# Recurrent gates in three split passes with their unit dealt anew, and four leading feed-forward pieces split ahead around the second norm

## The chip, the cores and the metric

The kernel runs on one core of one Trainium2 chip. The metric is the device time of that core in microseconds (us), the median of three runs. Engines are named as in the profile: PE is TensorE (matmul), PEld its weight loads, DVE VectorE, ACT ScalarE, POOL GpSimd and SP SyncE, which only starts DMAs here.

## The reference, cut to what matters

One layer over 256 tokens of width 2048, everything in fp32. A modulated RMSNorm feeds one input projection whose columns feed four token mixers. One of them is the recurrent unit (RG-LRU), computed for the tokens and for 256 context tokens, in both directions. The mixers are merged through sigmoid gates and one output projection. A second modulated RMSNorm follows, and then the feed-forward part.

```python
# recurrent unit: z is (tokens, 4 groups x 128), w_r and w_i are 4 blocks of 128x128 for each direction
r = sigmoid(block_diag_linear(z, w_r, b_r))
i = sigmoid(block_diag_linear(z, w_i, b_i))
log_a = -8.0 * r * softplus(-lam)
a = exp(log_a)
b = sqrt(-expm1(2.0 * log_a)) * (i * z)
h[t] = a[t] * h[t-1] + b[t]          # once forward, once backward

x_mixed = x + gt1 * (merged @ w_out)                          # out-projection, 2048 x 2048
h2 = (rms_norm(x_mixed) * g_ffn) * (1 + sc2) + sh2            # second norm
x = x_mixed + gt2 * ((silu(h2 @ w_ffn_gate) * (h2 @ w_ffn_up)) @ w_ffn_down)
```

## The kernel before, in words

**Split products.** PE multiplies fp32r operands. To keep fp32 accuracy every large operand is dealt into a high part (an ACT copy to fp32r) and a low part (a DVE subtraction, raw minus high), and each product is three passes: high by high, high by low, low by high (`rows3`, lines 1411 to 1413, and `piece_rows`, lines 1439 to 1441). Only small products, the recurrent gates among them, are plain fp32 matmuls (lines 1628 and 1629).

**Pieces.** All weights arrive in pieces of 256 x 512 (128 x 1024 on chip, 512 KB), numbered through the program. SP starts their DMAs into `RAW`, ACT writes `HI` (line 451, helper `high`), DVE writes `LO` (line 803, helper `low`). Each of the three buffers is a ring of four. `high(p)` waits for the landing and for PE to have finished piece p-4 (semaphore `used`), `low(p)` for `high(p)`, PE's piece p for `low(p)` (`ready`), and the DMA of piece p for `low(p-4)`. Small work is written into these streams by hand: `straight(w)` on ACT, DVE and PE is what comes behind piece w of the first 104. ACT and DVE work up to four pieces ahead of PE. An engine runs its stream in program order, so a wait holds back all that stands behind it.

**The recurrent unit.** For each of four groups g there is a unit placed at `LRU_AT[g]` (66, 73, 80, 87). DVE makes the convolution `Z` (a scale and three taps, 128x512 each) behind piece LRU_AT-3. PE runs four fp32 matmuls of 512 columns behind piece LRU_AT, two for each direction. ACT makes the sigmoids at +5 and +6, tanh and exp at +6 and +7, the square roots at +8 and +9. DVE makes i times z and two multiplications by (exp + 1) at +7 and +8 (lines 1058, 1060, 1061), the scans at +9 and +11, and the output is dealt by ACT at +12 and by DVE at +13.

**Around the second norm.** The out-projection is 32 pieces, eight (j = 0 to 7) for each of four column blocks n. In the last block, pieces j = 0 to 5 run for both token halves and pieces 6 and 7 first for half 0, then for half 1 (`row_pass`). `out_half` tells DVE that half 0 is complete. Then comes the chain of the norm for that half: DVE scales and adds the residual (`last_scaled`, `last_added`, lines 1216 and 1221), ACT squares the last 512 columns (line 706), DVE sums (1225), ACT takes the root (710), DVE takes the reciprocal and makes a diagonal (1229, 1230), and PE multiplies the residual stream by it, which turns and scales it at once (`h2_turn`, line 1803). The result is modulated and dealt in twelve units u: ACT's even column tile (718), DVE's odd one (1236, `h2_odd`), ACT's high part (721, `h2_high`), DVE's low part (903, `h2_low`). Units 0 to 3 are for token half 0 and units 4 to 7 for half 1 of the first eight column tiles; units 8 to 11 hold both halves of the other eight.

**The first feed-forward pieces.** I call pieces FFN0 to FFN0+15 f0 to f15; f0 to f7 are the gate weights of the first chunk. PE runs f0 to f3 by token halves, with `h2_turn` in between, and then f4 to f15 for both halves. Piece f4 waits for `h2_low` of unit 8, f5 for unit 9, f6 for unit 10 and f7 for unit 11 (PE waits for `h2_lo` at least w+5). In the streams of ACT and DVE, piece and unit are interlaced. For w = 4 to 9, DVE runs the odd part of unit w+2, the low part of piece fw and the low part of unit w+2; ACT runs `high(fw)` and then `h2_high(w+2)`. So the units stand two ahead of the pieces.

**What runs beside it.** POOL streams the modulation matrix, and DVE multiplies and adds its rows (line 915).

Of the kernel before, what the change touches and what calls it, by code (L numbers as in the profile page):

```python
# [104 lines left out]
LRU_AT = (66, 73, 80, 87)  # L105

# [27 lines left out]
def build(nc, x, c, ctx, c_ctx, w_mod, b_mod, g_mix, g_ffn, g_final, w_in, w_pool, pool_scale,  # L134
# [3 lines left out]
    with ctxs:  # L138
# [12 lines left out]
        Y = H[:, 0, :, :, :]  # L151
        HID = H[:, 0, 0:G4, :, :]
        HIDL = H[:, 0, G4:2 * G4, :, :]
        SUMS_HI = [[H[:, 0, 8 * g + n, :, :].rearrange("p l t -> p (l t)") for n in range(4)] for g in range(2)]
        SUMS_LO = [[H[:, 0, 8 * g + 4 + n, :, :].rearrange("p l t -> p (l t)") for n in range(4)] for g in range(2)]
# [58 lines left out]
        HS = BR[:, 11360:11616]  # L214
# [65 lines left out]
        def _(sp):  # L280
# [76 lines left out]
            for t in range(2):  # L357
                for n in (1, 0, 2, 3):
                    if n:
                        sp.wait_ge(s("rows_dve"), 3 * t + n)  # L360
                    else:
                        sp.wait_ge(s("rows_act"), t + 1)
                    sp.dma_start(out[0, t * P:(t + 1) * P, n * BW:(n + 1) * BW], OTOK[:, n, t, :]).then_inc(s(f"stored{t}"), 16)
            for t in range(2):
                sp.wait_ge(s(f"stored{t}"), 64)
# [77 lines left out]
        def _(act):  # L443
# [9 lines left out]
            act.dma_start(CST[:, :], cst).then_inc(s("cst_in"), 16)  # L453
            act.dma_start(CROW[0:KT, :], c[0].rearrange("(a n) -> a n", n=P)).then_inc(s("crow_in"), 16)
            act.dma_start(CROW[KT:2 * KT, :], c_ctx.rearrange("(a n) -> a n", n=P)).then_inc(s("crow_in"), 16)
# [106 lines left out]
            def straight(w):  # L562
# [43 lines left out]
                if w == SMALL_MM + 5:  # L606
                    act.wait_ge(s("sgu_float"), 1)
                    act.activation(Y[:, 4:8, 0, :], YF, ACT.Copy).then_inc(s("sgu_hi"), 1)
                if w == 70:
# [3 lines left out]
                for g in range(G4):  # L613
                    if w in (LRU_AT[g] + 5, LRU_AT[g] + 6):
                        for d in (w - LRU_AT[g] - 5,):
# [7 lines left out]
                            act.activation(LT[:, d, 0, :], ps[:, 4 + 2 * d, :], ACT.Sigmoid, bias=PB[:, PB_BR + col:PB_BR + col + 1]).then_inc(s("lru_r"), 1)  # L623
                            act.activation(LT[:, d, 1, :], ps[:, 5 + 2 * d, :], ACT.Sigmoid, bias=PB[:, PB_BI + col:PB_BI + col + 1]).then_inc(s("lru_i"), 1)
                    if w in (LRU_AT[g] + 6, LRU_AT[g] + 7):
                        for d in (w - LRU_AT[g] - 6,):
# [3 lines left out]
                            act.activation(LT[:, d, 2, :], LT[:, d, 0, :], ACT.Tanh, scale=LRC[:, 6, col:col + 1]).then_inc(s("lru_t"), 1)  # L630
                            act.activation(LT[:, d, 3, :], LT[:, d, 0, :], ACT.Exp, scale=LRC[:, 7, col:col + 1]).then_inc(s("lru_e"), 1)
# [4 lines left out]
                    if w == LRU_AT[g] + 12:  # L636
# [48 lines left out]
            def sums_high(g, n, src, groups):  # L685

                act.wait_ge(s("mod_used"), groups * KT + 2)
                act.activation(SUMS_HI[g][n], src, ACT.Copy).then_inc(s("sums_hi"), 1)

# [33 lines left out]
            high(FFN0 // 4, 0)  # L723
            high(FFN0 // 4, 1)
# [3 lines left out]
            high(FFN0 // 4, 2)  # L728
# [24 lines left out]
            for w in range(10, 16):  # L753
                high(FFN0 // 4, w)
                if w == 11:
                    ffn_gate(0, FFN0 + 7)
# [40 lines left out]
        def _(dve):  # L797
# [20 lines left out]
            dve.wait_ge(s("cst_in"), 16)  # L818
# [109 lines left out]
            def straight(w):  # L928
# [122 lines left out]
                for g in range(G4):  # L1051
                    if w in (LRU_AT[g] + 7, LRU_AT[g] + 8):
                        z = Z[:, g % 2, :]
                        for d in (w - LRU_AT[g] - 7,):
# [3 lines left out]
                            own.did(tt(I, I, z, ALU.mult))  # L1058
                            dve.wait_ge(s("lru_e"), n + 1)
                            own.did(stt(TH, EA, 1.0, TH, ALU.add, ALU.mult)); own.wait()  # L1060
                            stt(TH, EA, 1.0, TH, ALU.add, ALU.mult).then_inc(s("lru_w"), 1)
                    if w in (LRU_AT[g] + 9, LRU_AT[g] + 11):
                        for d in ((w - LRU_AT[g] - 9) // 2,):
                            n = 2 * g + d
                            R, I, TH, EA = (LT[:, d, k, :] for k in range(4))
                            dve.wait_ge(s("lru_s"), n + 1)
# [896 lines left out]
```

## Time and profile before

| | us |
|---|---|
| runs: median of 3 (lowest, highest) | 1635.61 (1634.35, 1636.22) |
| the profiled execution, its own time | 1635.51 |
| its span, first to last instruction | 1633.8 |
| PE busy in the span | 1603.9 |
| DVE busy | 1103.1 |
| ACT busy | 730.8 |

The 1.7 us between the execution's own time and its span lie around the span. A matmul is pipelined: a row gives its start and its whole latency, and the distance between the starts of neighbours is what it costs in a full stream.

### The profile page before, as it was taken

Reading aid. Unit: us, or ns where it says so; the run is one execution under the profiler, and the core shown is the slowest. Engines: PE = TensorE matmul, PEld = TensorE weight load, DVE = VectorE, ACT = ScalarE, POOL = GpSimd, SP = SyncE. Lnnn points to the kernel's source line nnn. Section 1 sums busy time; section 2 is a strip of 40 time slices with the busy share of each in tenths; the row PEclk is TensorE's granted clock in tenths of the full one; section 3 lists DMA queues with packets and bytes.
Section 4 is the critical chain, followed back from the end, with each engine's and each line's share of the span. In section 5 each row is a group of like instructions: output and inputs, shape, how many; then the busy total and the mean of one; then the engine's idle time right before and its main releaser. Section 6 shows DMA issues by size and latency. Waiting matters only on the chain.

```text
span 1633.8 us, 22715 instructions
## 1 busy us (share of the span) xinstructions
PE 1603.9 (98%) x7899; PEld 1322.8 (81%) x7899; DVE 1103.1 (68%) x1271; ACT 730.8 (45%) x820; POOL 159.6 (10%) x296
## 2 busy tenths in 40 slices
PE   6999999999999999999999999999999999999998
PEld 4678798987788888888887888888888888888886
DVE  4333556878888888877896576867755556456577
ACT  5333234468744444444445544443444444434444
POOL 1002111000022122123020010101100000000000
PEclk9999999999999999999999999999999999999999
DMA  9998746645589889899685677878776666666654
GB/s 346 356 357 245 243 144 203 222 147 156 187 298 326 282 297 337 278 340 341 220 287 164 179 235 244 280 233 268 248 254 193 191 193 187 188 191 191 190 174 139
DMA packets 200545, 390.28 MB, mean 239 GB/s; under 512 B 14400, under 2 KB 47408, under 8 KB 199584
## 3 DMA queue, kind: packets, MB, share of 16 engines
q1 hardware_dynamic: 176960, 312.51, 59.7%
q0 software_dynamic: 23312, 76.79, 14.1%
q8 instruction: 40, 0.66, 0.2%
q14 instruction: 25, 0.20, 0.0%
q10 hardware_dynamic: 208, 0.11, 0.0%
HBM read 386.35 MB, written 3.01 MB: 238 GB/s over the span
## 4 chain that ended last, share of the span: by engine, by line
PE 90%; DMA 5%; DVE 2%; issue 1%; ACT 1%; SPq 0%; POOL 0%; POOLq 0%; DVEq 0%; ACTq 0%
PE ps L1439 24%; PE ps L1441 24%; PE ps L1440 24%; PE ps L1411 5%; PE ps L1412 4%; PE ps L1413 4%; DMA BR<-in_w_mod 4%; PE ps L1407 2%; PE ps L1492 1%; DVE BR L915 1%; DMA MR<-in_w_mod 1%; DVE LO L803 1%; PE ps L1603 0%; PE ps L1590 0%; PE ps L1629 0%
## 5 line engine op out<-in xcount | busy, mean ns | idle before, releaser
L803 DVE TENSOR_TENSOR LO<-RAW,HI 128x1024 fp32r<-128x1024 f32 x519 | 633.0, 1223 | 399.5 <-ACT HI L451 398.3
L451 ACT ACTIVATE HI<-RAW 128x1024 fp32r<-128x1024 f32 x519 | 548.4, 1060 | 751.9 <-PE ps L1441 626.2
L1439 PE MATMUL ps<-HI,H 128*128 128x512 f32 x1840 | 720.6, 392 | 1.4 <-DVE ATT L1110 1.0
L1441 PE MATMUL ps<-HI,H 128*128 128x512 f32 x1840 | 716.4, 389 | 0.0
L1440 PE MATMUL ps<-LO,H 128*128 128x512 f32 x1840 | 716.0, 389 | 0.0
L1439 PEld LDWEIGHTS ps<-HI,H 128*128 128x128 f32 x1840 | 345.5, 188 | 74.5 <-DVE ATT L1110 1.4
L1441 PEld LDWEIGHTS ps<-HI,H 128*128 128x128 f32 x1840 | 345.4, 188 | 72.2
L1440 PEld LDWEIGHTS ps<-LO,H 128*128 128x128 f32 x1840 | 345.6, 188 | 72.0 <-issue 1.2
L413 POOL DMA_DIRECT2D BR<-in_w_mod x224 | 120.4, 538 | 765.2 <-DVE BR L915 306.4
L915 DVE SCALAR_TENSOR_TENSOR BR<-BR,SCF 128x512 f32<-128x512 f32 (+1 forms) x210 | 156.7, 746 | 12.7 <-DMA BR<-in_w_mod 10.8
L1411 PE MATMUL ps<-H,HI 128*128 128x256 f32 (+1 forms) x384 | 125.7, 327 | 0.1
L1412 PE MATMUL ps<-H,HI 128*128 128x256 f32 (+1 forms) x384 | 122.9, 320 | 0.0
L1413 PE MATMUL ps<-H,LO 128*128 128x256 f32 (+1 forms) x384 | 122.7, 320 | 0.0
L1411 PEld LDWEIGHTS ps<-H,HI 128*128 128x128 f32 x384 | 73.4, 191 | 11.0 <-issue 5.4
L1412 PEld LDWEIGHTS ps<-H,HI 128*128 128x128 f32 x384 | 73.5, 191 | 5.3 <-issue 0.2
L1413 PEld LDWEIGHTS ps<-H,LO 128*128 128x128 f32 x384 | 73.4, 191 | 5.3
L1289 DVE TENSOR_TENSOR ATT<-ps,ATT 128x1024 f32<-128x1024 f32 x36 | 43.8, 1216 | 0.0
L1411 PE MATMUL ps<-HI,H 128*128 128x512 f32 x80 | 32.3, 404 | 2.0 <-DVE H L903 2.0
L1492 PE MATMUL ps<-BR 128*32 128x256 f32 x400 | 26.7, 384 | 5.4 <-DMA BR<-in_w_mod 5.4
L1412 PE MATMUL ps<-LO,H 128*128 128x512 f32 x80 | 31.3, 391 | 0.0
L1413 PE MATMUL ps<-HI,H 128*128 128x512 f32 x80 | 31.2, 390 | 0.0
L1407 PE MATMUL ps<-CST,BR 128*128 128x128 f32 (+1 forms) x129 | 19.4, 303 | 11.7 <-DMA BR<-in_c_ctx 8.5
(258 smaller groups left out, 759.2 us busy)
## 6 DMA issues: line engine op xcount, KB each, us to landing
RAW<-in_w_gate SPq DMA_DIRECT2D x128, 512.0 KB, 4.7
BR<-in_w_mod POOLq DMA_DIRECT2D x224, 256.0 KB, 4.6
RAW<-in_w_ffn_gate SPq DMA_DIRECT2D x88, 512.0 KB, 3.8
RAW<-in_w_ffn_up SPq DMA_DIRECT2D x88, 512.0 KB, 3.7
RAW<-in_w_ffn_down SPq DMA_DIRECT2D x88, 512.0 KB, 3.7
RAW<-in_w_in SPq DMA_DIRECT2D x64, 512.0 KB, 5.7
BR<-in_w_mod SPq DMA_DIRECT2D x50, 512.0 KB, 9.4
RAW<-in_w_branch SPq DMA_DIRECT2D x32, 512.0 KB, 5.2
```

Source lines behind the costliest of these rows:

```text
L413: pool.dma_start(slots[:, k % ring, :], w_mod[0, k * P:(k + 1) * P, bass.ds(g * BW + first, BW)])\
L451: act.activation(HI[:, j % RING, :], RAW[:, j % RING, :], ACT.Copy).then_inc(hi_done, 1)
L803: tt(LO[:, j % RING, :], RAW[:, j % RING, :], HI[:, j % RING, :], ALU.subtract).then_inc(lo_done, 1)
L915: i = stt(acc, src, SCF[:, 0, k:k + 1], acc, ALU.mult, ALU.add)
L1289: tt(flat(ACC[:, n, :]), pair(4 + 2 * (n % 2)), flat(ACC[:, n, :]), ALU.add).then_inc(s("down_read"), 1)
L1407: return mm(o, src, IDENT[0:n, 0:n], start=start, stop=True, is_transpose=True, skip_group_check=True)
L1411: mm(o, wh, xh, start=first, stop=False, skip_group_check=True)
L1412: mm(o, wh, xl, start=False, stop=False, skip_group_check=True)
L1413: return mm(o, wl, xh, start=False, stop=last, skip_group_check=True)
L1439: mm(o, xh, wh, start=first and t == 0, stop=False, skip_group_check=True)
L1440: mm(o, xh, wl, start=False, stop=False, skip_group_check=True)
L1441: i = mm(o, xl, wh, start=False, stop=last and t == 1, skip_group_check=True)
```

## The change: what it does

1. **Gates in three passes.** The weights of the gates are dealt into high (ACT, behind pieces 53, 55, 56 and 59, one group of 128x512 each) and low (DVE, four pieces later). `Z` of each unit is dealt too: high by ACT at LRU_AT-2, low by DVE at LRU_AT-1. PE runs `rows3` in place of each fp32 matmul, and waits for both low parts.
2. **The unit dealt anew.** The convolution moves to LRU_AT-6 (scale, first tap) and LRU_AT-4 (two taps). ACT takes the root right behind the tanh, without waiting for DVE. DVE then multiplies by (exp + 1) once, at +9 and +10, in place of twice. The output is dealt one piece later (+13, +14).
3. **Pieces f0 to f3 ahead.** They are dealt out of `RAW` into eight free rows of `H` (`AHEAD_HI`, `AHEAD_LO`) and not into the ring, so that they no longer wait for ring slots. Then f4 to f7 take the ring slots as the pieces of the out-projection leave them (`high_behind`).
4. **Token halves.** The last four pieces of the out-projection (j = 4 to 7) run by token halves, not the last two, and the first `h2_turn` stands behind piece 6 of the second half.
5. **Order of ACT and DVE behind that.** Written anew, see the diff: for u = 8 to 11, unit u and then piece fu.
6. Some semaphores are merged: DVE's first reduction waits for three constants' DMAs and not for one, and SP's last waits are one.

```diff
+LRU_SPLIT_AT = (53, 55, 56, 59)
...
+        GATES_HI = Y[:, 8:12, :, :].rearrange("p g l (h n) -> p g l h n", h=2)
+        ROWS = [H[:, 0, k, :, :].rearrange("p l t -> p (l t)") for k in range(KT)]
+        AHEAD = [H[:, 0, k:k + 2, :, :].rearrange("p k l t -> p (k l t)") for k in (8, 10, 12, 14, 2, 4, 6, 0)]
+        AHEAD_HI, AHEAD_LO = AHEAD[0::2], AHEAD[1::2]
...
# ACT, straight(w)
+                if w in LRU_SPLIT_AT:
+                    g = LRU_SPLIT_AT.index(w)
+                    act.wait_ge(s("small_in"), 16 * 7)
+                    act.wait_ge(used, 8 * 3 + 8 + 4)
+                    act.activation(GATES_HI[:, g], GATES[:, g], ACT.Copy).then_inc(s("gates_hi"), 1)
+                if w + 2 in LRU_AT:
+                    g = LRU_AT.index(w + 2)
+                    act.wait_ge(s("conv"), g + 1)
...
+                    act.activation(ZH, Z[:, g % 2, :], ACT.Copy).then_inc(s("conv_hi"), 1)
...
-                            act.wait_ge(s("lru_w"), 2 * g + d + 1)
+                            act.wait_ge(s("lru_t"), 2 * g + d + 1)
                             act.activation(LT[:, d, 2, :], LT[:, d, 2, :], ACT.Sqrt).then_inc(s("lru_s"), 1)
...
# ACT, second norm
-            high(FFN0 // 4, 0)
-            high(FFN0 // 4, 1)
+            def high_ahead(w):
+                act.wait_ge(landed[w], FFN0 // 4 * 16 + 16)
+                if w == 2:
+                    act.wait_ge(s("gate1_spread"), 1)
+                act.activation(AHEAD_HI[w], RAW[:, w, :], ACT.Copy).then_inc(hi_done, 1)
+            def high_behind(w):
+                act.wait_ge(landed[w % RING], FFN0 // 4 * 16 + 32)
+                act.wait_ge(used, FFN0 + w - 3)
+                act.activation(HI[:, w % RING, :], RAW[:, w % RING, :], ACT.Copy).then_inc(hi_done, 1)
+            for w in range(4):
+                high_ahead(w)
             act.activation(ST[:, 62:63], EPSC[:, 0:1], ACT.Sqrt)
             square_last(0)
             root(0)
-            high(FFN0 // 4, 2)
+            high_behind(4)
             act.wait_ge(s("a2"), 1)
             h2_high(0)
             h2_high(1)
-            high(FFN0 // 4, 3)
+            square_last(1)
             h2_high(2)
-            square_last(1)
+            root(1)
             h2_high(3)
-            root(1)
+            high_behind(5)
             h2_high(4)
             h2_high(5)
-            for w in range(4, 10):
-                high(FFN0 // 4, w)
-                h2_high(w + 2)
+            high_behind(6)
+            h2_high(6)
+            high_behind(7)
+            h2_high(7)
+            for u in range(8, 12):
+                h2_high(u)
+                high(FFN0 // 4, u)
...
# DVE, straight(w)
-                            own.did(tt(I, I, z, ALU.mult))
+                            tt(I, I, z, ALU.mult).then_inc(s("lru_w"), 1)
+                    if w in (LRU_AT[g] + 9, LRU_AT[g] + 10):
...
                             own.did(stt(TH, EA, 1.0, TH, ALU.add, ALU.mult)); own.wait()
-                            stt(TH, EA, 1.0, TH, ALU.add, ALU.mult).then_inc(s("lru_w"), 1)
...
+                if w - 4 in LRU_SPLIT_AT:
+                    g = LRU_SPLIT_AT.index(w - 4)
+                    split_low("gates_hi", g + 1, GATES_LO[:, g], GATES[:, g], GATES_HI[:, g], "gates_lo")
+                if w + 1 in LRU_AT:
...
+                    split_low("conv_hi", g + 1, ZL, Z[:, g % 2, :], ZH, "conv_lo")
...
# DVE, second norm
+            def low_ahead(w):
+                dve.wait_ge(hi_done, FFN0 + w + 1)
+                if w >= 2:
+                    dve.wait_ge(s("gate1_spread"), w - 1)
+                tt(AHEAD_LO[w], RAW[:, w, :], AHEAD_HI[w], ALU.subtract).then_inc(lo_done, 1)
-            low(FFN0, 0)
-            low(FFN0 + 1, 1)
+            low_ahead(0)
+            low_ahead(1)
             last_scaled(0)
             last_added(0)
+            low_ahead(2)
             squares_summed(0)
             rstd_diagonal(0)
+            low_ahead(3)
             h2_odd(0)
             h2_odd(1)
             h2_low(0)
-            h2_odd(2)
             h2_low(1)
-            low(FFN0 + 2, 2)
             last_scaled(1)
             last_added(1)
+            h2_odd(2)
+            h2_odd(3)
             h2_low(2)
-            h2_odd(3)
-            low(FFN0 + 3, 3)
             squares_summed(1)
             h2_low(3)
             rstd_diagonal(1)
-            for u in (4, 5):
+            low(FFN0 + 4, 4)
+            low(FFN0 + 5, 5)
+            for u in (4, 5, 6, 7):
                 h2_odd(u)
                 h2_low(u)
-            for w in range(4, 10):
-                h2_odd(w + 2)
-                low(FFN0 + w, w)
-                h2_low(w + 2)
+                if u >= 6:
+                    low(FFN0 + u, u)
+            for u in range(8, 12):
+                h2_odd(u)
+                h2_low(u)
+                low(FFN0 + u, u)
...
# PE
-                            mm(ps[:, 4 + 2 * d, :], SW[:, 8 + 4 * d + g, :], Z[:, g % 2, :], start=True, stop=True)
-                            mm(ps[:, 5 + 2 * d, :], SW[:, 16 + 4 * d + g, :], Z[:, g % 2, :], start=True, stop=True)\
+                            rows3(ps[:, 4 + 2 * d, :], GATES_HI[:, g, 0, d, :], GATES_LO[:, g, 0, d, :], ZH, ZL, True, True)
+                            rows3(ps[:, 5 + 2 * d, :], GATES_HI[:, g, 1, d, :], GATES_LO[:, g, 1, d, :], ZH, ZL, True, True)\
                                 .then_inc(s("lru_mm"), 1)
...
-                for j in range(8 if n < 3 else 6):
+                for j in range(8 if n < 3 else 4):
...
             for q in range(2):
-                for j in (6, 7):
-                    i = row_pass(OUT0 + 24 + j, j, tokens_of(HX), q, ps[:, 2 + q, :], 2 * j, False, j == 7)
+                for j in range(4, 8):
+                    i = row_pass(OUT0 + 24 + j, HI[:, j % RING, :], LO[:, j % RING, :], tokens_of(HX), q, ps[:, 2 + q, :],
+                                 2 * j, False, j == 7)
+                    if q and j == 6:
+                        h2_turn(0)
                 if q == 0:
-                    i.then_inc(s("out_half"), 1)
-
-            h2_turn(0)
+                    i.then_inc(s("half_done"), 1)
+
             h2_turn(1)
```

## Rows read from the trace of the kernel before

**Rows 1.** The page, part 1: busy time, share of the span, instructions.

```profile
PE 1603.9 (98%) x7899; PEld 1322.8 (81%) x7899; DVE 1103.1 (68%) x1271; ACT 730.8 (45%) x820; POOL 159.6 (10%) x296
```

**Rows 2.** Waits of PE over the span: us in total, times, longest.

```profile
PE ps L1407 <- DMA BR<-in_c_ctx: 8.5, 1, 8.5
PE ps L1411 <- DVE H L903: 2.0, 4, 0.6
PE ps L1439 <- DVE ATT L1110: 1.0, 1, 1.0
```

**Rows 3.** Chain of waits around the first recurrent unit: start, us, what.

```profile
344.98 0.86 PE ps L1628 x2
348.41 0.23 PE ps L1439
```

**Rows 4.** Timeline of ACT, DVE and PE behind piece f4.

```profile
908.71 0.39 PE L1439 MATMUL ps<-HI,H 128*128 128x512 f32 x1
908.97 1.06 ACT L451 ACTIVATE HI<-RAW 128x1024 fp32r<-128x1024 f32 x1 [2.02 <-PE ps L1441]
910.06 1.23 DVE L803 TENSOR_TENSOR LO<-RAW,HI 128x1024 fp32r<-128x1024 f32 x1 [1.78 <-ACT HI L451]
911.20 0.68 DVE L903 TENSOR_TENSOR H<-BR,H 128x512 fp32r<-128x512 f32 x1
911.80 0.54 DVE L1236 TENSOR_SCALAR BR<-ps,A,MC 128x256 f32<-128x256 f32 x1
911.94 0.50 PE L1439 MATMUL ps<-HI,H 128*128 128x512 f32 x1 [0.35 <-DVE H L903]
913.23 0.63 ACT L721 ACTIVATE H<-BR 128x512 fp32r<-128x512 f32 x1
914.82 0.39 PE L1439 MATMUL ps<-HI,H 128*128 128x512 f32 x1
917.54 0.39 PE L1439 MATMUL ps<-HI,H 128*128 128x512 f32 x1
```

**Rows 5.** Groups by line, DVE, 340 to 440 us: busy, mean ns, idle.

```profile
L1061 DVE SCALAR_TENSOR_TENSOR ATT<-ATT 128x512 f32<-128x512 f32 x8 | 5.5, 692 | 0.3
```

**Rows 6.** Timeline before the units: start, us, line, [idle and who ended it].

```profile
315.39 2.35 DVE L803 TENSOR_TENSOR LO<-RAW,HI 128x1024 fp32r<-128x1024 f32 x2
318.98 1.06 ACT L451 ACTIVATE HI<-RAW 128x1024 fp32r<-128x1024 f32 x1 [1.82 <-PE ps L1413]
```

**Rows 7.** Timeline of DVE, ACT and PE from the end of the out-projection to piece f4.

```profile
873.99 1.23 DVE L803 TENSOR_TENSOR LO<-RAW,HI 128x1024 fp32r<-128x1024 f32 x1 [1.96 <-ACT HI L451]
879.41 1.28 ACT L725 ACT_TABLE_LOAD   x1
881.00 0.69 DVE L1216 TENSOR_TENSOR ATT<-ps,ACCM 128x512 f32<-128x512 f32 x1 [0.34 <-PE ps L1413]
882.44 0.63 ACT L706 ACTIVATE ATT<-BR 128x512 f32<-128x512 f32 x1 [1.53 <-DVE BR L1221]
884.26 2.05 PE L1803 MATMUL ps<-ATT,BR 128*128 128x128 f32 x16 [0.58 <-DVE ATT L1230]
905.86 0.47 PE L1439 MATMUL ps<-HI,H 128*128 128x512 f32 x1
```

**Rows 8.** The page, part 6: DMA issues, size, us from issue to landing.

```profile
RAW<-in_w_ffn_gate SPq DMA_DIRECT2D x88, 512.0 KB, 3.8
```

**Rows 9.** Windows: PE, PEld, DVE, ACT, POOL busy (count), PE clock, DMA, GB/s.

```profile
883.52:905.86 22.34, 19.75 (x113) 16.10 (x113) 15.18 (x31) 14.54 (x29) 0.00 (x0) 1.00 0.34 97
28.00:32.00 4.00, 1.25 (x12) 0.71 (x12) 2.42 (x7) 2.77 (x6) 0.00 (x0) 1.00 1.07 360
32.00:36.00 4.00, 3.65 (x15) 2.61 (x16) 2.51 (x3) 1.78 (x3) 0.00 (x0) 0.60 1.10 351
```

**Rows 10.** Chain of waits where the clock was low: start, us, what.

```profile
34.20 0.43 PE ps L1413
```

**Rows 11.** Timeline of DVE at the start.

```profile
8.86 0.16 DVE L874 RECIPROCAL ST<-ST 128x1 f32<-128x1 f32 x1 [1.99 <-ACT ST L493]
```

More of the change, by code:

```diff
@@ L362, in _ @@
                         sp.wait_ge(s("rows_act"), t + 1)
-                    sp.dma_start(out[0, t * P:(t + 1) * P, n * BW:(n + 1) * BW], OTOK[:, n, t, :]).then_inc(s(f"stored{t}"), 16)
-            for t in range(2):
-                sp.wait_ge(s(f"stored{t}"), 64)
+                    sp.dma_start(out[0, t * P:(t + 1) * P, n * BW:(n + 1) * BW], OTOK[:, n, t, :]).then_inc(s("stored"), 16)
+            sp.wait_ge(s("stored"), 128)
         @block.gpsimd
@@ L1081, in straight @@
                         tt(HS, HS, LG[:, g * T:g * T + T], ALU.mult).then_inc(s("lru_float"), 1)
-                    if w == LRU_AT[g] + 13:
+                    if w == LRU_AT[g] + 14:
                         split_low("lru_hi", g + 1, Y[:, 8 + g, 1, :], HS, Y[:, 8 + g, 0, :], "lru_lo")
-                if w + 3 in LRU_AT:
-                    g = LRU_AT.index(w + 3)
-                    z = Z[:, g % 2, :].rearrange("p (s t) -> p s t", s=2)
-                    dve.wait_ge(s("win_read"), 2)
-                    if g == 0:
-                        dve.wait_ge(s("pooled"), 1)
-                    if g >= 2:
-                        dve.wait_ge(s("lru_w"), 2 * (g - 1))
-                    own.did(ts(z, LP[:, g, :, 0:T], PB[:, PB_CW + g:PB_CW + g + 1], PB[:, PB_CB + g:PB_CB + g + 1], ALU.mult, ALU.add))
-                    for k in range(1, CONV):
+                if w - 4 in LRU_SPLIT_AT:
+                    g = LRU_SPLIT_AT.index(w - 4)
+                    split_low("gates_hi", g + 1, GATES_LO[:, g], GATES[:, g], GATES_HI[:, g], "gates_lo")
+                if w + 1 in LRU_AT:
+                    g = LRU_AT.index(w + 1)
+                    if g:
+                        dve.wait_ge(s("lru_mm"), 2 * g)
+                    else:
+                        dve.wait_ge(s("sgu_mm"), 1)
+                    split_low("conv_hi", g + 1, ZL, Z[:, g % 2, :], ZH, "conv_lo")
+                for g in range(G4):
+                    if w not in (LRU_AT[g] - 6, LRU_AT[g] - 4):
+                        continue
+                    z = Z[:, g % 2, :].rearrange("p (s t) -> p s t", s=2)
+                    if w == LRU_AT[g] - 6:
+                        dve.wait_ge(s("win_read"), 2)
+                        if g == 0:
+                            dve.wait_ge(s("pooled"), 1)
+                        if g >= 2:
+                            dve.wait_ge(s("lru_w"), 2 * (g - 1))
+                        own.did(ts(z, LP[:, g, :, 0:T], PB[:, PB_CW + g:PB_CW + g + 1], PB[:, PB_CB + g:PB_CB + g + 1], ALU.mult, ALU.add))
+                        taps = (1,)
+                    else:
+                        taps = (2, 3)
+                    for k in taps:
                         own.wait()
@@ L1164, in sums_low @@
             def sums_low(g, n, src):
+                if g == 0 and n == 3:
+                    dve.wait_ge(s("gate1_spread"), 1)
                 split_low("sums_hi", 4 * g + n + 1, SUMS_LO[g][n], src, SUMS_HI[g][n], "sums_lo")
@@ L1363, in _ @@
                 if w == 21:
-                    dve.memset(ST[:, 3:4], EPS).then_inc(s("eps_set"), 1)
-                    dve.memset(ST[:, 7:8], EPS).then_inc(s("eps_set"), 1)
+                    own.did(dve.memset(ST[:, 3:4], EPS))
+                    own.did(dve.memset(ST[:, 7:8], EPS))
                 if w == 25:
@@ L1386, in last_rows @@
                     dve.wait_ge(s("sqf"), 6)
-                    dve.wait_ge(s("eps_set"), 2)
+                    own.wait()
                     for u in range(2):
@@ L1776, in gate1_spread, with row_pass @@
                 i.then_inc(s("gate1_spread"), 1)
-            def row_pass(p, j, lhs, q, o, k0, first, last):
+            def row_pass(p, hi, lo, lhs, q, o, k0, first, last):
                 ready(p)
                 for t in range(2):
-                    wh, wl = HI[:, j % RING, t * BW:(t + 1) * BW], LO[:, j % RING, t * BW:(t + 1) * BW]
+                    wh, wl = hi[:, t * BW:(t + 1) * BW], lo[:, t * BW:(t + 1) * BW]
                     xh, xl = lhs(k0 + t, q)
```

63 lines of the change are left out of this document (38 added, 25 removed).

## The prediction

> **What bounds the kernel now.** I read the page first. PE is busy 98% of the span, DVE 68%, ACT 45% [rows 1], and the chain of waits is 90% PE. So whatever PE is spared, and whatever wait is put in front of it, shows in the time nearly one to one; work of ACT and DVE counts only where PE waits for it. Next the list of PE's waits: behind the first 60 us there is hardly one, except around the second norm, where PE waits for DVE's line 903 (low parts of units), four times, 2.0 us in all [rows 2]. That is the place the change rewrites. Last I read the timelines of ACT, DVE and PE side by side there, since both streams are written by hand and run in order: what a stream waits for matters as much as how long its work takes.
>
> **Gates in three passes.** A unit of four fp32 matmuls takes 348.41 - 344.98 = 3.43 us, 0.86 each [rows 3]. An fp32r pass of 512 columns in a full stream costs 2.72 us / 12 = 0.227 us (914.82 to 917.54 is one piece of 12 matmuls) [rows 4]. A unit becomes 12 passes: 2.72 us, 0.71 less. Four units: -2.8 us. All of it is on PE's path. Both ends: the twelve passes may cost 0.23 to 0.24 each where weights change every pass, so -2.2 to -2.9.
>
> **What the dealing costs.** DVE gets eight subtractions of 128x512 (gates and Z) and loses eight multiplications of the same size at 0.69 us [rows 5]: even. ACT gets eight copies, each like its square of 128x512, 0.63 us [rows 7], where it idles 1 to 2 us behind each piece. The tight place is before the units, where pooling and normalization keep DVE late: the low parts of pieces 59 and 60 end at 317.7 (315.39 + 2.35), the first of them at 316.5, and PE takes piece 59 up at 318.9, when piece 58 is done [rows 6]. In front of piece 59 the change puts one subtraction (0.6 us): the lead falls from 2.4 to 1.7 us and holds. Two more and the first half of the convolution (some 1.3 us) come in front of piece 61, where PE arrives two pieces later. I take 0; if the cover fails, some tenths, up to 1 us. Inside the units the root no longer waits for DVE and the low part of Z is written several pieces ahead: 0. The output is dealt one piece later, with several pieces to spare before the fourth branch group.
>
> **The end of the out-projection.** Half 0 is complete two half passes earlier, 2 x 1.36 = 2.7 us, so DVE's residual can start at 878.3 in place of 881.0 [rows 7]. The chain of the norm then waits for something else: ACT's stream. Four early high parts now stand in front of the table load. The fourth needs the DMA of f3, which starts when the low part of the last out-projection piece is written, 873.99 + 1.23 = 875.2 [rows 7], and lands 3.8 us later at 879.0 [rows 8]. Then 1.1 for the high part, 1.28 for the table load and 0.2 for its instruction: the square comes at 881.7, not 882.44, 0.75 earlier. From square to turn is 884.26 - 882.44 = 1.82 [rows 7], so `h2_turn` starts at 883.5. But PE stands before it at 882.2 (883.5 less the half pass that was moved behind it) and waits 1.3 us where it waited 0.7. That pass then covers the first units. I follow the streams down to f4 with a half pass at 1.36 (0.1 more behind a wait), a turn group of the norm at 0.85, and the durations of ACT and DVE in these rows: turn 883.5, half pass 884.4, turn 885.8, f0 886.6; f2 waits 0.9 for unit 2, which stands behind the residual and the square of half 1, until 890.4; f3 waits 0.2, until 892.1; the turns of half 1 from 893.6; f0 of half 1 waits 0.9 for unit 4 (two low parts of pieces stand before it in DVE's queue), until 896.2; a turn from 899.0, f2 900.7, the last turn 903.6, f4 905.3, where the trace has 905.86: -0.6. The stretch has 22.34 - 19.75 = 2.6 us in which PE is idle [rows 9]; that is the most the step can win. It can lose about 1. I take -0.6.
>
> **Pieces f4 to f7, the step that decides.** Ring slot 0 holds f4, so the high part of f8 can't be written before PE is done with f4. Before, DVE's order was odd part of unit w+2, low part of piece w, low part of unit w+2: when DVE stood waiting for f8, unit 9 was long dealt and unit 10 half done. So f5 found its unit ready, and f6 (unit 10) waited 0.5 us: 911.94 against 911.43 [rows 4]. Now the order is unit u, then piece fu. DVE writes unit 8 and then waits for f8, hence for the end of f4; unit 9 stands behind it in the queue. PE, done with f4, needs unit 9 for f5. ACT has the same order. The same repeats: unit 10 stands behind f9 (end of f5), unit 11 behind f10 (end of f6). So PE waits a full chain before f5, f6 and f7. The chain, from the instant when PE could start the next piece (908.71 in the trace) [rows 4]: 0.26 to the high part of f8 (908.97), 1.09 to its low part (910.06), 1.14 until DVE is free (911.20), the odd part of the unit 0.54, a handover of 0.1, ACT's high part 0.63, 0.03, DVE's low part 0.68, 0.06 to PE. Sum 4.53 us. Nothing hides any link, since each waits for the one before it and the first waits for PE itself.
>
> From f4 to f8 before: 917.54 - 905.86 = 11.7 us. After: 2.85 for f4, three times (4.53 + 2.88), the piece with its slower first pass: 25.1. The difference is +13.4 for this stretch. The 2.88 is f6 behind its wait, 914.82 - 911.94 [rows 4]. Both ends: each wait 4.2 to 4.8, so +12.4 to +14.2. Behind f8 the high and low parts of f8 to f10 exist already and the streams catch up within two pieces: 0.
>
> **PE's clock in these waits.** The trace has one loss of clock after the start. In the window 28 to 32 us PE is busy 1.25 us of 4, and in the next one the granted clock is 0.60 on average [rows 9], that is 1.2 GHz for some 3 us: seven matmuls start 0.43 us apart [rows 10], not 0.227, a loss of 7 x 0.2 = 1.4 us. The idle stretches of 0.6 to 1.8 us elsewhere cost no clock. The new waits, 4.3 us of idle, lie between, nearer to the one that did. Bounds: 0, or one such loss for each wait, 4.2, or, if the 2.8 us pieces between waits do not bring it back, 12 x 0.2 + 12 x 0.2 + 1.4 = 6.2. I take 1.8, a bit more than one loss. The Trainium skill, "TensorE: Matmul & The Clock Gate", section "HAM oscillation — how this bites in real kernels", describes this pattern: short bursts between waits of this length each start on the low clock, every time. By that rule the term is 4.2 or more and the time about 1650. No run here shows it for waits of 4.3 us.
>
> **Elsewhere.** PE's one other wait of the long middle, 1.0 us for line 1110 [rows 2], ends a stage in which DVE waits for the modulation stream; that chain starts from PE's own pieces, so it moves with them: 0, give or take 0.5.
>
> **Start and end.** DVE's first reduction now waits for the constants that PE waits for until 8.47 [rows 2]; it takes 0.2 us, and DVE's next instruction is at 8.86 anyway [rows 11]. I take 0, at most 0.2. SP's last wait: 0.
>
> **Sum.** Against the profiled execution (1635.5 us of its own, 1.7 of it around the span; the median of the runs is 1635.6, so no correction): -2.8 - 0.6 + 13.4 + 1.8 = +11.8. Time 1647.3.
>
> **Rivals.**
> The clock falls in every wait (the rule above, as a mechanism of this kernel: f5, f6 and f7 each begin at 1.2 GHz): -2.8 - 0.6 + 13.4 + 4.2 = +14.2, 1649.7; with no recovery inside a piece 1651.7. For it: 4.3 us of idle. Against: the one fall in the trace came after 5 us that were nearly empty.
> The waits before f5 to f7 don't exist (the other side, faster). Its place is DVE's queue at unit 9: it decides from the point where unit 9 to 11 are dealt before PE ends f4, which needs them ahead of the piece in program order. Then only the gains remain, and the 0.6 of f6 too: -2.8 - 0.6 - 0.6 = -4.0, 1631.5. For it: the ahead pieces do free ACT and DVE by about 3 us before f4. Against: the order in the code; time alone can't help, as the wait is for PE.
> The gate unit gives nothing: its passes wait for a low part, or the lead before piece 59 is lost. The gain of 2.8 goes, the waits stay: 1650.1. Against: leads of several pieces.
> The waits are partly hidden and the gains larger, which together end near no change (1635 to 1641). I see no cover for a wait that is for PE itself.
>
> **Chances.** Forecast (three chains, clock lost in part, 1645.5 to 1649) 0.62; clock lost in all 0.17; gates give nothing 0.10; faster 0.06; near no change 0.05, of which 0.03 is within 0.2%. 0.2% is 3.3 us, about what a measurement of this kernel can tell. Faster 0.06, same 0.03, slower 0.91. Range 1642 to 1652.
>
> **What the profile will show.** Right: three idle stretches of PE of about 4.2 us before f5, f6 and f7, ended by line 903 of DVE, each with ACT's high part starting 0.1 us after PE stopped; units of recurrent gates 2.7 us long; no wait of PE between 290 and 440 us; `h2_turn` at a wait of about 1.3. The granted clock between f5 and f8 says which clock case holds. Wrong: if f5 starts right behind f4, my reading of the order is wrong and the time is below 1633.

## The result, and the profile after

| | us, median of the runs | ratio to before, 95% interval |
|---|---|---|
| before | 1635.91 (1634.35 to 1637.9) | |
| after | 1651.39 (1650.78 to 1655.12) | 1.0099 (1.0087 to 1.0111) |

The ratios here and below are estimated from all the runs and need not be the quotients of the medians. By the medians the kernel became slower by 15.5 us. The forecast was 1647.3, with 1642 to 1652 as its range. The profiled execution after took 1651.08 us with a span of 1649.4, so the spans differ by 15.6 us and can be compared directly.

The page's first part, after (busy time, share of the span, instructions; answers to [rows 1]):

```profile
PE 1607.7 (97%) x7915; PEld 1329.3 (81%) x7915; DVE 1103.5 (67%) x1271; ACT 734.3 (45%) x828; POOL 159.6 (10%) x296
```

PE is still the bound, with one per cent of the span lost. The list of PE's waits, after (who waited for whom: us in total, times, longest; answers to [rows 2]). Lines have moved: line 944 was 903 (low part of a unit), 844 was 803 (low part of a piece), 1511 to 1513 are the three passes of a piece for both token halves, 1483 to 1485 the passes of `rows3`, 1875 is the norm's turn. Kernels of the experiments with added lines shift these numbers again by one to five (the first pass of a piece is line 1513 in e2 and 1516 in e1):

```profile
PE ps L1511 <- DVE H L944: 13.1, 3, 4.4
PE ps L1483 <- DVE H L944: 1.2, 2, 0.6
PE ps L1483 <- DVE LO L844: 0.9, 1, 0.9
PE ps L1875 <- DVE ATT L1292: 0.8, 1, 0.8
```

The first row is new: three waits of 4.4 us. The second is what is left of the four waits of 2.0 us in all. The third is new as well, and the 1.0 us for line 1110 is gone; of these two more is said below.

PE's timeline behind piece f4, after (start, us, line, operation, [idle and who ended it]; answers to [rows 4]):

```profile
901.78 0.48 PE L1511 MATMUL ps<-HI,H 128*128 128x512 f32 x1
...
904.37 0.39 PE L1513 MATMUL ps<-HI,H 128*128 128x512 f32 x1
909.12 0.80 PE L1511 MATMUL ps<-HI,H 128*128 128x512 f32 x1 [4.37 <-DVE H L944]
909.72 0.63 PE L1512 MATMUL ps<-LO,H 128*128 128x512 f32 x1
910.14 0.63 PE L1513 MATMUL ps<-HI,H 128*128 128x512 f32 x1
...
913.98 0.63 PE L1513 MATMUL ps<-HI,H 128*128 128x512 f32 x1
918.98 0.79 PE L1511 MATMUL ps<-HI,H 128*128 128x512 f32 x1 [4.37 <-DVE H L944]
...
928.84 0.80 PE L1511 MATMUL ps<-HI,H 128*128 128x512 f32 x1 [4.37 <-DVE H L944]
...
931.99 0.41 PE L1512 MATMUL ps<-LO,H 128*128 128x512 f32 x1
...
933.15 0.39 PE L1511 MATMUL ps<-HI,H 128*128 128x512 f32 x1
```

Read it in two passes. First the brackets: f5, f6 and f7 each begin behind 4.37 us of idle that DVE's low part of their unit ended. Then the starts: behind a wait the passes are 0.427 us apart (909.72, 910.14), not 0.227. In f5 and f6 it stays so to the end of the piece; in f7 it ends after three microseconds.

The chain of waits between f4 and f5, after (start, us, what):

```profile
904.53 0.24 PE ps L1513
...
904.85 1.06 ACT HI L459
905.94 1.23 DVE LO L844
907.17 0.47 DVE BR L1298
...
907.72 0.64 ACT H L746
908.38 0.70 DVE H L944
...
909.12 0.80 PE ps L1511
```

This is the sum of the prediction, link by link: PE's end frees the ring slot, ACT writes the high part of f8, DVE its low part, then DVE the odd part of unit 9, ACT its high part, DVE its low part. The same links follow f5 (from 914.71) and f6 (from 924.56).

Windows of the stretch, after (busy us and counts of PE, PEld, DVE, ACT, POOL; granted clock; DMA; GB/s):

```profile
909.00:914.00 5.00, 4.88 (x12) 3.81 (x12) 0.07 (x1) 0.00 (x0) 0.00 (x0) 0.50 0.22 82
...
919.00:924.00 5.00, 5.00 (x12) 3.77 (x12) 0.00 (x0) 0.00 (x0) 0.00 (x0) 0.50 0.24 89
...
929.00:934.00 5.00, 5.00 (x16) 4.01 (x17) 0.00 (x0) 0.59 (x1) 0.00 (x0) 0.70 0.19 73
```

The clock column is 0.50 while f5 and f6 run, that is 1.2 GHz, and PE is 98 to 100% "busy" in them. The same 12 matmuls take 5.3 us there and 2.9 us in [rows 4]; the busy column alone would not show it.

Two windows inside the idle stretch between f5 and f6, after (PE busy and count; clock; DMA; GB/s):

```profile
915.00:918.00 3.00, 0.00 (x0) 1.00 0.00 0
918.00:918.50 0.50, 0.00 (x0) 0.83 1.26 102
```

The last pass of f5 ended at 914.6 by the profile. The granted clock is full again from 915.0 on, with PE idle, and falls once more before f6 starts. So f6 is not slow because the low clock was carried over from f5: each wait loses the clock anew, and it came back too late to serve f5. It is the same between f6 and f7.

Where the 15.6 us came from, by the start of the same work on PE in both traces:

| stretch, by its end on PE | after minus before, us |
|---|---|
| four recurrent units, 0.65 each | -2.6 |
| before piece 55, a wait that was not there | +1.0 |
| the wait for line 1110, which is gone, and small change | -1.4 |
| end of the out-projection to f4 | -1.1 |
| f4 to f8: 31.37 (901.78 to 933.15) against 11.68 [rows 4, 7] | +19.7 |
| sum | +15.6 |

Of the 19.7 the waits are 13.4: a wait costs 4.52 us (the pass of 0.227 behind 904.37 would have been followed at 904.60, and f5 came at 909.12). The low clock is 6.3: f5 and f6 each 5.29 us (909.12 to 914.41, which is 913.98 and one step of 0.427) where 2.88 is the piece at full clock with its slower first pass, and f7 4.31 (928.84 to 933.15). 2.41 + 2.41 + 1.43 = 6.25.

### The profile page after: what moved, and what is told of

Same layout as the page of the kernel before. It is cut to its first block, busy times and chain, and to the rows that moved or that the text cites. A ratio compares the mean times of both kernels' runs of the same rounds, so it can differ in the third digit from the quotient of the medians.

```text
span 1649.4 us, 22782 instructions
## 1 busy us (share of the span) xinstructions
PE 1607.7 (97%) x7915; PEld 1329.3 (81%) x7915; DVE 1103.5 (67%) x1271; ACT 734.3 (45%) x828; POOL 159.6 (10%) x296
## 4 chain that ended last, share of the span: by engine, by line
PE 93%; DMA 3%; ACT 2%; DVE 1%; issue 0%; SPq 0%; DVEq 0%; POOLq 0%; ACTq 0%
PE ps L1511 25%; PE ps L1513 25%; PE ps L1512 25%; PE ps L1483 4%; PE ps L1485 4%; PE ps L1484 4%; PE ps L1479 1%; DMA MR<-in_w_mod 1%; PE ps L1563 1%; DMA BR<-in_w_mod 1%; PE ps L1674 0%; PE ps L1661 0%; DVE LO L844 0%; ACT ATT L498 0%; PE ps L1875 0%
## 5 line engine op out<-in xcount | busy, mean ns | idle before, releaser
L459 ACT ACTIVATE HI<-RAW 128x1024 fp32r<-128x1024 f32 x511 | 540.3, 1060 | 764.2 <-PE ps L1513 651.0
L1511 PE MATMUL ps<-HI,H 128*128 128x512 f32 x1832 | 718.6, 392 | 13.1 <-DVE H L944 13.1
L1513 PE MATMUL ps<-HI,H 128*128 128x512 f32 x1832 | 715.6, 391 | 0.0
L1512 PE MATMUL ps<-LO,H 128*128 128x512 f32 x1832 | 715.4, 390 | 0.0
L421 POOL DMA_DIRECT2D MR<-in_w_mod x32 | 17.5, 549 | 117.1 <-DVE ACCM L956 103.2
L956 DVE SCALAR_TENSOR_TENSOR ACCM<-MR,SCF,ACCM 128x512 f32<-128x512 f32 x30 | 22.4, 748 | 9.5 <-DMA MR<-in_w_mod 9.5
L1483 PE MATMUL ps<-HI,H 128*128 128x512 f32 x72 | 28.6, 398 | 0.0
```

The costliest lines, as they stand in the source:

```text
L421: pool.dma_start(slots[:, k % ring, :], w_mod[0, k * P:(k + 1) * P, bass.ds(g * BW + first, BW)])\
L459: act.activation(HI[:, j % RING, :], RAW[:, j % RING, :], ACT.Copy).then_inc(hi_done, 1)
L956: i = stt(acc, src, SCF[:, 0, k:k + 1], acc, ALU.mult, ALU.add)
L1483: mm(o, wh, xh, start=first, stop=False, skip_group_check=True)
L1511: mm(o, xh, wh, start=first and t == 0, stop=False, skip_group_check=True)
L1512: mm(o, xh, wl, start=False, stop=False, skip_group_check=True)
```

## The experiments

e1 to e4 compare with 27 runs of the kernel before, median 1635.82 us, e5 to e8 with 15 runs of it on another chip, 1635.53. They stand here in the order of their questions, behind the row of the kernel after from above.

| kernel | us, median | ratio, 95% interval | stretch of the second norm |
|---|---|---|---|
| after | 1651.39 | 1.0099 (1.0087 to 1.0111) | unit u, then piece fu |
| e1 | 1634.32 | 0.9992 (0.9983 to 1.0002) | units one ahead of the pieces |
| e2 | 1631.36 | 0.9975 (0.9966 to 0.9984) | units 8 to 11 ahead of f8 to f11 |
| e3 | 1646.05 | 1.0062 (1.0046 to 1.0077) | as after, waits filled, 18 matmuls each |
| e7 | 1645.34 | 1.0060 (1.0041 to 1.0078) | as after, 8 matmuls in each wait |
| e8 | 1651.48 | 1.0097 (1.0079 to 1.0116) | as after, 4 matmuls in each wait |
| e4 | 1633.19 | 0.9981 (0.9972 to 0.9990) | as before; the gates of the change |
| e6 | 1632.30 | 0.9980 (0.9971 to 0.9989) | e2, fewer token halves |
| e5 | 1629.41 | 0.9961 (0.9948 to 0.9975) | e2, the norm's chain first |

### Is it the order, and how far ahead must a unit be? (e1, e2)

The theory: f5 to f7 wait since their unit is queued behind a piece that waits for PE. The rival: DVE and ACT have too much to do in this stretch, and would be late in any order. e2 deals the four units first; nothing is added or removed. In ACT's stream, and alike in DVE's:

```diff
             for u in range(8, 12):
                 h2_high(u)
+            for u in range(8, 12):
                 high(FFN0 // 4, u)
```

> The changed kernel with units 8 to 11 all ahead of pieces f8 to f11 on ACT and DVE. My theory: no wait before f5, f6 and f7, the stretch f4 to f8 is 10.9 to 11.1 us, no fall of the clock, the high part of f8 is late by nothing that PE sees. Time 1651.4 - 20.3 = 1631.1, faster than the kernel before (1635.9) by 4.8. Rival (DVE's load decides): four units one behind the other take DVE and ACT over 5 us, f5 or f6 waits 1 to 3 us, time 1633 to 1635.

1631.36 us: 20.0 below the kernel after by moving loop bodies. PE's timeline of e2, first passes of f4, f5 and f6:

```profile
903.10 0.48 PE L1513 MATMUL ps<-HI,H 128*128 128x512 f32 x1
...
905.91 0.39 PE L1513 MATMUL ps<-HI,H 128*128 128x512 f32 x1
...
908.63 0.39 PE L1513 MATMUL ps<-HI,H 128*128 128x512 f32 x1
```

There is no bracket and each piece follows 2.72 us behind the last. The granted clock is 1.00 from 904 to 934 us. The rival is out: both engines have the time. e1 puts each unit one piece ahead only (unit 9, f8, unit 10, f9, unit 11, f10):

```diff
+            h2_high(8)
-            for u in range(8, 12):
+            for u in range(9, 12):
                 h2_high(u)
-                high(FFN0 // 4, u)
+                high(FFN0 // 4, u - 1)
+            high(FFN0 // 4, 11)
```

> The changed kernel with one edit: on ACT and DVE the units stand one ahead of the pieces (unit 8, unit 9, f8, unit 10, f9, unit 11, f10, f11). My theory (the three waits come from the order unit u, then piece fu, as f8 needs the end of f4, and the low clock comes from these waits): no wait before f5; before f6 one chain less the piece f5, 4.5 - 2.7 = 1.8 us; before f7 none. The stretch f4 to f8 is 10.9 + 1.8 + 0.1 = 12.8 us, not 31.4, and the clock stays at 2.4 GHz, since 1.8 us of idle cost no clock elsewhere. Time 1651.4 - 18.6 = 1632.8. Rival (the units are late because DVE has too much to do there, not because of the order): the waits go down by less than half and the time stays above 1642.

1634.32 us, 1.5 above what was expected, and too near the kernel before for its interval to tell them apart (0.9983 to 1.0002). PE's timeline of e1 has one wait that the theory gave (1.8 expected; 909.75 stands in place of 907.94, so 1.81) and one that it did not:

```profile
909.75 0.50 PE L1516 MATMUL ps<-HI,H 128*128 128x512 f32 x1 [1.66 <-DVE H L946]
...
913.14 0.50 PE L1516 MATMUL ps<-HI,H 128*128 128x512 f32 x1 [0.37 <-DVE H L946]
```

ACT's timeline of e1 tells why (the high part of f9):

```profile
908.88 1.04 ACT L459 ACTIVATE HI<-RAW 128x1024 fp32r<-128x1024 f32 x1
```

PE ended f5 at 907.94 (its last pass started at 907.71), but ACT stood in the high part of unit 10 and took up f9 at 908.88, 0.94 us later. The chain to unit 11 then took 4.26 us more and ended at 913.14, where PE would have been at 912.6. The expectation had started the second chain from PE's end alone; the first chain's delay is handed on. With its slower first passes the second wait accounts for 0.7 of the 1.5 us; the rest stays open (the spans of the profiled executions of e1 and e2 differ by 1.9 us, the medians by 3.0). A lead of one piece hides 2.7 us of a chain of 4.5, a lead of all four hides it.

### Is the rest of the loss the clock? (e3, e7, e8)

After, the three waits stand beside a loss of 6.3 us in slow pitch. The theory: that is the clock, lost by idleness, so work without use in the wait brings it back while the wait keeps its length. The rival: a pass behind such a wait is slow for another reason (weight loads, data that comes late), and filling changes nothing.

```diff
             for w in range(4, 16):
+                if w in (5, 6, 7):
+                    pe.wait_ge(s("xm_new"), 5)
+                    for _ in range(18):
+                        mm(ps[:, 2, :], HX[:, 0, 0, 0:P], AHEAD_HI[0][:, 0:BW], start=True, stop=True, skip_group_check=True)
```

> The changed kernel with 18 matmuls of 512 columns into an unused bank in front of each of PE's three waits (before f5, f6 and f7); their results aren't used. The waits stay as long as they were, but PE works in them. My theory (the clock falls because PE stands idle 4.4 us, and that costs 6.3 us): f5 to f7 run at 0.227 us a pass, the time falls by some 6 us to 1645.2, a sum of -2.6 (gates), -1.1, -1.4 and +13.6 (three waits) against the kernel before. Rival (the clock is a state of its own there, or the work of these pieces runs slow for another reason): no change, 1651.4, or slower by the added work.

1646.05 us, 5.3 below the kernel after. Its profiled execution was the longest of its four (1648.39), with 1.9 us of waiting in the modulation stage, so its rows are read and its span is not. PE's timeline of e3:

```profile
908.17 4.24 PE L1920 MATMUL ps<-H 128*128 128x512 f32 x18
912.71 0.50 PE L1511 MATMUL ps<-HI,H 128*128 128x512 f32 x1 [0.30 <-DVE H L944]
913.05 0.40 PE L1512 MATMUL ps<-LO,H 128*128 128x512 f32 x1
913.29 0.40 PE L1513 MATMUL ps<-HI,H 128*128 128x512 f32 x1
```

The wait is as long as before (4.5 us from the end of the piece) and the pitch behind it is 0.24, not 0.43. The rival is out. e7 and e8 have 8 and 4 matmuls in place of 18, to see how much idleness it takes.

> The changed kernel with 8 matmuls in front of each of PE's three waits (in e3 there were 18), so that PE stands idle about 2.6 us in each. Two readings of the clock: if an idle stretch of 2.6 us keeps it, as those of up to 1.8 us do in the kernel before, the time is that of e3, 1645.5 to 1646; if it falls, f5 to f7 start at 1.2 GHz and the time is up to 6 us longer, to 1651.4. I expect the first, 1646.

> The same with 4 matmuls: idle about 3.5 us in each wait. 1646 if the clock stays, 1651.4 if it falls in all three, between them if in some. I expect that it falls in some, 1648.5.

e7, PE's timeline at the first wait and the window behind it (PE's columns alone: busy, count, clock, DMA, GB/s):

```profile
905.03 1.98 PE L1920 MATMUL ps<-H 128*128 128x512 f32 x8
909.57 0.50 PE L1511 MATMUL ps<-HI,H 128*128 128x512 f32 x1 [2.56 <-DVE H L944]
909.90 0.39 PE L1512 MATMUL ps<-LO,H 128*128 128x512 f32 x1
```

```profile
909.00:914.00 5.00, 4.43 (x19) 1.00 0.31 102
```

e8, the same views, with the first passes behind the second and the third wait:

```profile
906.05 1.07 PE L1920 MATMUL ps<-H 128*128 128x512 f32 x4
910.58 0.79 PE L1511 MATMUL ps<-HI,H 128*128 128x512 f32 x1 [3.47 <-DVE H L944]
911.17 0.63 PE L1512 MATMUL ps<-LO,H 128*128 128x512 f32 x1
...
920.43 0.79 PE L1511 MATMUL ps<-HI,H 128*128 128x512 f32 x1 [3.27 <-DVE H L944]
...
930.29 0.79 PE L1511 MATMUL ps<-HI,H 128*128 128x512 f32 x1 [3.11 <-DVE H L944]
```

```profile
909.00:914.00 5.00, 3.42 (x8) 0.55 0.36 105
```

In the second and third wait of e8 the added matmuls began at the low clock and got it back before they ended, at about 916.3 and 926.5, and it fell again. e7 is at 1645.34, with all three waits at full clock; e8 at 1651.48, the time of the kernel after, with all three at 1.2 GHz behind them. Four matmuls fewer cost 6.1 us. So the clock's share is 6.0 us (after less e7), and the three waits alone are e7 less e2, 14.0 us (two chips, whose medians of the kernel before differ by 0.3). The expectation for e8 was 1648.5 and is a miss: it had some of the waits keep the clock, and none did. Each of e7 and e8 has only two runs, and the intervals of their ratios just miss each other (up to 1.0078, from 1.0079). The traces are the firmer evidence: from the first pass of f4 to that of f8 it is 25.1 us in e3, 25.0 in e7, 31.4 in e8 and 31.4 in the kernel after, so the clock's share there is 6.3.

Is it the length of the idle stretch alone? e8, two windows inside its first wait:

```profile
909.00:909.50 0.50, 0.00 (x0) 0.97 0.00 0
909.50:910.00 0.50, 0.00 (x0) 0.50 0.73 66
```

The four added matmuls ended at 907.1, so the clock fell 2.4 us into the idle stretch. In e7 PE stood idle for 2.56 us, three times, and the granted clock is 1.00 from 904 to 928 us. A shorter idle stretch lost the clock here and a longer one kept it, so the length alone doesn't set it; what else does, no run was made to find.

### What are the gates and the rest of the norm worth? (e4)

e4 keeps the recurrent part of the change and takes back all of the second norm: high and low parts in the ring, units two ahead of the pieces as before, the half passes of the last out-projection pieces as before. In DVE's stream:

```diff
-            for u in range(8, 12):
-                h2_odd(u)
-                h2_low(u)
-                low(FFN0 + u, u)
+            for w in range(4, 10):
+                h2_odd(w + 2)
+                low(FFN0 + w, w)
+                h2_low(w + 2)
```

> The recurrent unit's part of the change alone: the streams around the second norm are those of the kernel before. My theory: each unit of gates 0.65 us shorter, no new wait of PE, together -2.6 us; the wait of 1.0 us for DVE's merge near 780 us and the one before piece 55 near 304 us hang on when the modulation rows land and can add or take 1.0 each. Time 1633.3, between 1632.3 and 1634.3. Rival (the dealing costs what the passes save): 1635.9.

1633.19 us, 2.6 below before. The unit itself, in PE's timeline after (first pass of the unit, first pass of the next piece; answers to [rows 3]):

```profile
345.83 0.40 PE L1483 MATMUL ps<-BRR,H 128*128 128x512 f32 x1
...
348.61 0.40 PE L1511 MATMUL ps<-HI,H 128*128 128x512 f32 x1
```

2.78 us where it was 3.43: four times 0.65 is 2.6, all of what e4 gained. The dealing took nothing back, as the theory had it. And e2 less e4 is -1.8 us, which is what the early pieces and the token halves bring once the order is mended.

### Can the norm's own chain be shortened? (e6, e5)

In e2 the first turn of the norm waits 1.3 us. Two ways to ease that: fewer passes by halves (then half 0 of the residual is complete later, but less is moved behind the norm), or ACT's stream in another order. e6:

```diff
-                for j in range(8 if n < 3 else 4):
+                for j in range(8 if n < 3 else 6):
...
-                for j in range(4, 8):
+                for j in range(6, 8):
```

> As e2, but only the last two pieces of the out-projection run by token halves, as in the kernel before; the first turn still stands behind piece 6 of half 1. My theory: half 0 is complete 2.7 us later, so the norm's chain is no longer held up by ACT's early high parts but by PE itself; the first turn waits about 1.3 us longer. Time 1632.6. Rival (ACT's stream sets the start of the square in both, so four halves bring nothing): 1631.4.

1632.30 us, 0.9 above e2: the wait became longer. PE's timeline of e6 and then of e2 at that turn:

```profile
882.10 1.75 PE L1877 MATMUL ps<-ATT,BR 128*128 128x128 f32 x8 [2.20 <-DVE ATT L1293]
```

```profile
881.51 1.16 PE L1877 MATMUL ps<-ATT,BR 128*128 128x128 f32 x8 [1.34 <-DVE ATT L1293]
```

The intervals of the two ratios overlap, so the medians alone don't settle this; the wait does. The six kernels with four pieces by halves and this order of ACT's stream (after, e1, e2, e3, e7, e8) show 0.7 to 1.4 us there in their profiles, e6 2.2. Four pieces by halves are better than two. e5 leaves them, and takes the fourth early high part from in front of the norm's table load and puts it behind the root of half 0; in both streams the units of half 0 come before the square and root of half 1:

```diff
-            for w in range(4):
+            for w in range(3):
                 high_ahead(w)
...
+            high_ahead(3)
             high_behind(4)
...
-            square_last(1)
             h2_high(2)
-            root(1)
             h2_high(3)
+            square_last(1)
+            root(1)
```

> Units 8 to 11 ahead of f8 to f11 as in e2, and two more edits to the streams: ACT takes the table load, the square and the root of half 0 before the early high part of f3 (whose DMA it had to await), and units 2 and 3 stand ahead of the square of half 1 on ACT and are interlaced with its residual on DVE. My theory: PE's wait before the first turn (0.84 to 1.3 us) goes, as the square can start at about 876.8 and not 878.4, and the waits before f2 and f3 (0.6 and 0.1, with slow first passes 1.2 in all) go; only the 0.6 before f0 of the second half stays. Time 1631.4 - 2.1 = 1629.3. Rival (the chain is then held up elsewhere, by the low part of f3 in DVE's queue or by the late diagonal of half 1): 1630.5 to 1631.5.

1629.41 us, 6.1 below before and 22.0 below after. ACT's timeline of e5 around the square of half 0, and PE's only wait for a unit:

```profile
877.78 0.63 ACT L731 ACTIVATE ATT<-BR 128x512 f32<-128x512 f32 x1 [0.69 <-DVE BR L1285]
```

```profile
891.37 0.53 PE L1486 MATMUL ps<-H 128*128 128x512 f32 x1 [0.58 <-DVE H L946]
```

The square now waits for DVE's residual, as its bracket says, not for ACT's own queue; in the kernel after it stood behind a fourth high part and the table load and came at 878.36 with no bracket. Counted from the start of DVE's residual for half 0, the square comes 1.45 us later in e5 (876.33 to 877.78) and 3.07 us later in the kernel after (875.29 to 878.36). PE has no wait at the first turn left, and one wait of 0.6 us for a unit where e2 has two. e5 makes both edits at once: by PE's waits 1.3 of the 2.0 us below e2 are the turn's and 0.6 the unit's, but no run parts them. This is the best version of all.

## Why the prediction was right or wrong

**The order of the streams: right.** Three waits before f5, f6 and f7, each for DVE's low part of a unit, each with ACT's high part starting 0.1 us after PE stopped. A wait was put at 4.53 us and measured 4.52. e2 shows the cause by taking it away: the faster rival, 1631.5 with the units ahead of the piece in program order, is near what e2 measured (1631.36). That it is so near is in part luck: the rival's gains add up to -4.0 from 1635.5, e2 lies 4.5 below its own runs of the kernel before.

**PE's clock in these waits: the step that was mis-sized.** "I take 1.8, a bit more than one loss." This term of the sum measured 6.3 in the trace and 6.0 between the medians of e7 and after: the clock fell in each of the three waits, and in two of them it stayed low for the whole piece behind. The prediction's own outer bound was 6.2, by its worst case: f5 and f6 at 1.2 GHz to their end, f7 for a part, and the rival built on it said 1651.7 against 1651.39 measured; its other parts were off by 0.2 to 0.5 us each and cancelled in part, so the last tenths are luck. What failed was the weighing. The argument against was that the one loss in the trace came behind 5 us that were nearly empty, and the new waits are 4.3 us. But 0.6 to 1.8 us without a loss and 5 with one say nothing of 4.3, and "a bit more than one loss" for three waits of equal length has no case behind it: the three waits are alike in length and in what PE does before them, and no row tells one from the others. The losses came three times of three, 2.41, 2.41 and 1.43 us. The sentence on the Trainium skill, "TensorE: Matmul & The Clock Gate", section "HAM oscillation — how this bites in real kernels", was right here: short bursts between waits of this length start on the low clock every time, and this trace agrees, three times of three (0.50 in the windows of f5 and f6, and 0.43 us from pass to pass at the start of f7), and e8 three more times.

**Gates in three passes: right.** -2.8 forecast, -2.6 measured, inside its bounds: 2.78 us for twelve passes, 0.232 each. **The dealing: right at 0.** No unit waits for a low part, and e4 has the whole gain.

**The end of the out-projection: right in sign, low in size.** -0.6 forecast, -1.1 measured. The stream of ACT did set the time of the square, as worked out: f3's high part waited 1.35 us for its DMA, then came the table load. But the first turn waited 0.8 us, not 1.3, and the later units 0.6 twice, where 0.9, 0.2 and 0.9 had been forecast.

ACT's timeline after, before the square:

```profile
875.88 1.06 ACT L753 ACTIVATE H<-RAW 128x1024 fp32r<-128x1024 f32 x1 [1.35 <-DMA RAW<-in_w_ffn_gate]
876.96 1.28 ACT L763 ACT_TABLE_LOAD   x1
878.36 0.62 ACT L731 ACTIVATE ATT<-BR 128x512 f32<-128x512 f32 x1
```

**Elsewhere, 0 give or take 0.5: the sum was near, its parts were not.** The 1.0 us for line 1110 is gone, and 0.9 us of waiting came before piece 55, where the prediction had said that PE would not wait between 290 and 440 us. The chain of waits after, in front of piece 55:

```profile
296.01 3.68 DMA MR<-in_w_mod
...
304.69 0.38 PE ps L1483
```

It starts at a DMA of the modulation rows. The same two waits turn up in different sizes in the profiles of other kernels of this study whose code there is the same: before piece 55 1.0 us in e5, 0.8 in e3, 0.7 in e6 and e7, 0.4 in e4 and e8, 0.3 in e1 and none in e2; for the line-1110 kind 0.5 in e5, 0.4 in e2, 0.3 in e4. A third one, for a low part of a piece between 700 and 730 us, is not there in the kernels before and after and in e5, takes 0.2 to 0.5 us in e1, e4, e6 and e7, 0.9 in e2, 1.5 in e8 and 1.9 in e3. They look like chance of the DMA from one execution to the next, but no run was made to show that, so it stays open. A difference of one or two microseconds between the spans of two profiled executions is therefore no measure of an edit.

**The sum.** -2.6 - 1.1 + 13.4 + 6.3 - 0.4 = +15.6. With the clock at its measured 6.3 the forecast would have been 1651.8, 0.4 above the median measured.

## What to carry to other kernels

In streams that run in order, ask of every item what it waits for, not only how long it takes: a small item that PE needs next must not stand behind one that waits for PE to finish now, and one piece of lead only hides one piece's time (13.4 us of waits with no lead, 2.3 with one piece, none with four, for the same work). When a change makes PE stand idle several times, each for as long as here (3.1 to 4.4 us), charge each wait with the low clock behind it as well, here 1.4 to 2.4 us on top of 4.5; and where the wait can't be removed, even a few matmuls without use in it can pay (8 of them gave back 6.0 us, 4 gave nothing). A chain is best started by placing its first instruction ahead of early work on the same engine, as e5 did with the square (the turn's wait of 1.3 us in e2 is gone).

## What the runs showed of the hardware

- All waits with 2.56 us of idle (e7, three) kept 2.4 GHz; all with 3.11, 3.27, 3.47 (e8) and 4.37 us (after, three) lost it. But in e8 the clock fell 2.4, 2.5 and 2.8 us after PE had stopped, in the kernel after 3.3, 3.7 and 4.1, so the length of the idle stretch alone doesn't set the moment.
- Regaining it took different times: f5 and f6 of the kernel after ran all 12 matmuls, 5.3 us, at 1.2 GHz, and the clock was full again 0.3 and 0.7 us after the piece had ended, with PE idle; so did f5 and f6 of e8, where it came back in the added matmuls behind them. f7 was back at full pitch 3.1 us after its start in both. From each fall to the rise behind it the clock was low for 6.8, 6.8 and 3.4 us in the kernel after and in e8 alike. The prediction took f7's kind from the start of the kernel [rows 9, 10] and had f5's only as a bound.
- Behind a wait at full clock the first pass starts the next one 0.33 us later and the rest are 0.23 apart (e7: 909.57, 909.90, 910.13), a surcharge of 0.1 us. It is not the waiting alone that costs it: behind a turn of the norm, with no wait, it is the same (f4 in the kernel after: 901.78 to 902.10).
